# A routed-expert encoder layer: experts add their gated rows into the residual in DRAM, and the last stage only normalises

## What is computed

```python
h = h + parallel_mixer(...)                       # called H2 in the kernel
u = rms_norm(h, norm_ffn_g)                       # called U2
gates = p_grp * (top_p / sum(top_p))              # two experts a token
# tokens sorted by expert, each expert's list padded to blocks of 128 slots
def run_block(args):
    tok, e = args
    xe = x[tok]
    hid = silu(xe @ w_gate[e]) * (xe @ w_up[e])
    return hid @ w_down[e]
y = zeros((T, D)).at[buf_tok].add(yb.reshape(P, D) * buf_gate[:, None])
out = rms_norm(h + y, norm_final_g)
```

## Time and profile before

| | |
|---|---|
| median of 3 runs | 4235.22 us (4228.05 to 4240.24) |
| the profiled execution's own time | 4237.25 us |
| its span, first to last instruction | 4235.1 us |
| attention | from about 540 to 2890 us |
| route | 3291 to 3356 us |
| experts | 3356 to 4060 us |
| combine | 4060.5 to 4235.1 us |
| PE busy in the span | 88% |
| mean granted TensorE clock | 0.935 of full speed |

### The profile page before, as it was taken

One profiled execution on the slowest core, in us unless ns is written; L12 is line 12 of the kernel. 1 busy time (PEld: TensorE's weight loads), 2 busy tenths in 40 slices (PEclk: granted clock), 3 DMA queues, 4 the chain that ended last, 5 costly groups with the idle time before them and its releaser, 6 DMA issues. The chain is left out here.

```text
span 4235.1 us, 60176 instructions
## 1 busy us (share of the span) xinstructions
PE 3738.5 (88%) x16747; PEld 2738.7 (65%) x16748; DVE 2819.2 (67%) x4468; ACT 2366.1 (56%) x4059; POOL 429.1 (10%) x497
## 2 busy tenths in 40 slices
PE   7999856999999999999999999996999499999920
PEld 7989724666666666666666766765777366666610
DVE  5656545888878888777776877743443666666645
ACT  4434303777777777776676766784332155555522
POOL 0000010111111111111011011000000011110123
PEclk9999957999999999999999999998999699999965
DMA  4555574221222211221122022003333277777768
GB/s 161 167 194 194 166 166 160 60 46 26 54 60 60 59 40 28 60 59 42 24 59 60 16 48 60 6 7 141 137 125 113 84 254 249 248 248 248 248 211 295
DMA packets 330198, 495.54 MB, mean 117 GB/s; under 512 B 118791, under 2 KB 261411, under 8 KB 318915
## 3 DMA queue, kind: packets, MB, share of 16 engines
q1 hardware_dynamic: 241798, 359.85, 28.8%
q10 hardware_dynamic: 71888, 73.54, 5.0%
q0 software_dynamic: 16272, 59.25, 4.1%
HBM read 330.84 MB, written 161.78 MB: 116 GB/s over the span
## 5 line engine op out<-in xcount | busy, mean ns | idle before, releaser
L940 ACT ACTIVATE b_p_hi<-b_psS 128x512 fp32r<-128x512 f32 (+1 forms) x1376 | 822.1, 597 | 620.2 <-PE b_psS L1071 579.5
L1071 PE MATMUL b_psS<-b_q,b_k 96*128 96x512 f32 (+3 forms) x3440 | 1053.2, 404 | 53.5 <-ACT b_prob L943 31.6
L988 DVE TENSOR_TENSOR b_p_lo<-b_prob,b_p_hi 128x512 fp32r<-128x512 f32 x1152 | 830.1, 722 | 287.5 <-ACT b_prob L943 248.5
L943 ACT ACTIVATE b_prob<-b_psS 128x512 f32<-128x512 f32 (+1 forms) x1376 | 815.1, 592 | 1.1
L1071 PEld LDWEIGHTS b_psS<-b_q,b_k 96*128 96x128 f32 (+3 forms) x3440 | 629.8, 186 | 285.0 <-ACT b_prob L943 39.2
L996 DVE TENSOR_REDUCE b_mx_s<-b_psM 128x1 f32<-128x512 f32 x1024 | 690.8, 687 | 86.8 <-PE b_psM L1102 66.1
L1102 PE MATMUL b_psM<-b_k,b_q 128*128 128x512 f32 (+1 forms) x1280 | 515.8, 424 | 54.5 <-DMA b_v<-V 39.2
L1094 PE MATMUL b_psO<-b_p_hi,b_v_hi 128*65 128x512 f32 x1280 | 516.9, 404 | 25.8 <-DVE b_p_lo L988 23.9
L1094 PE MATMUL b_psO<-b_p_hi,b_v_lo 128*65 128x512 f32 x1280 | 509.7, 398 | 0.0
L1094 PE MATMUL b_psO<-b_p_lo,b_v_hi 128*65 128x512 f32 x1280 | 509.6, 398 | 0.0
L1102 PEld LDWEIGHTS b_psM<-b_k,b_q 128*128 128x128 f32 (+1 forms) x1280 | 251.8, 197 | 158.2 <-DVE b_mx_s L996 53.1
(11 more groups left out here) (246 smaller groups left out, 5184.9 us busy)
## 6 DMA issues: line engine op xcount, KB each, us to landing
e_w_gu<-w_gate SPq DMA_DIRECT2D x32, 1024.0 KB
e_w_gu<-w_up SPq DMA_DIRECT2D x32, 1024.0 KB
e_w_dn<-w_down SPq DMA_DIRECT2D x32, 1024.0 KB
Y<-e_y ACTq DMA_DIRECT2D x64, 512.0 KB, 5.3
Y<-b_zeros ACTq DMA_DIRECT2D x4, 4096.0 KB, 27.3
a_x_raw<-xallT SPq DMA_DIRECT2D x25, 512.0 KB, 5.0
a_x<-xall SPq DMA_DIRECT2D x25, 512.0 KB, 4.4
c_o<-O SPq DMA_DIRECT2D x24, 512.0 KB, 4.9
```

The lines of the kernel that those rows point to most:

```text
L940: nc.scalar.activation(p_hi[0:kn, (s * NI + j) % NP, :], psS[0:kn, j % 2, :], ACT.Exp)
L943: nc.scalar.activation(prob[0:kn, (s * NI + j) % NP, :], psS[0:kn, j % 2, :], ACT.Exp).then_inc(p_ready, 1)
L988: nc.vector.tensor_tensor(out, prob[0:kn, slot, :], p_hi[0:kn, slot, :].bitcast(F32), ALU.subtract).then_inc(lo_ready, 1)
L1071: m = nc.tensor.matmul(psS[0:kn, j % 2, :], kk[s][0:r, k], qq[s][0:r, q], start=n == 0, stop=n == len(passes) - 1)
```

## The change

`Y` is gone. The residual H2 takes its place as the target: for each block, once its rows are multiplied by their gates, POOL issues an indirect store of 128 rows of 4 KB that adds to the rows of H2 in DRAM. H2 and U2 get 128 rows ahead of the tokens' rows. A slot that only pads a block has token number 0 in `psI` and gets its own row number (0 to 127) instead, so that no row is named twice in one store; its gate is 0. Since a token occurs in two experts' blocks, an add waits until the one before has landed.

- Attention: instead of four stores of 4096 KB there are eight of 128 KB, which clear the new rows of U2 and H2.
- Route: `in_blk` holds two sets of 80 columns, one scaled by the token's number, one by its gate. PE's products have 160 columns, and the result also gives `gates`, per block and row.
- Experts: ACT copies a column of `gates` to `gcur` and scales by it while it takes `psY` out. POOL no longer waits for the landing of its gather, but issues the adds, each four blocks behind the gather ahead of it in its queue. A new count `y_landed` tells ACT that a buffer of `y` is free.
- Combine: SP loads H2 alone, eight tiles deep; ACT and DVE normalise, four results deep.

The core of the diff:

```diff
             for c in range(D // 256):
-                act.dma_start(t["Y"].rearrange("(b p) d -> p b d", p=P)[:, BLOCKS_SURE:, c * 256:c * 256 + 256],
-                              zeros[:, :].unsqueeze(1).broadcast_to([P, BLOCKS - BLOCKS_SURE, 256])).then_inc(y_cleared, 16)
+                for name in ("U2", "H2"):
+                    act.dma_start(t[name][0:P, c * 256:c * 256 + 256], zeros[:, :]).then_inc(cleared_rows, 16)
...
-                        i = nc.tensor.matmul(psI[:, 0:BLOCKS], in_row[:, k, n, :], in_blk[:, k, n, :],
+                        i = nc.tensor.matmul(psI[:, 0:2 * BLOCKS], in_row[:, k, n, :], in_blk[:, k, n, :, :].rearrange("p a b -> p (a b)"),
...
-                    nc.vector.tensor_tensor(in_blk[:, k, part, :], in_blk[:, k, part, :],
-                                            tok[:, part].unsqueeze(2).broadcast_to([P, HN, BLOCKS]),
+                    nc.vector.tensor_tensor(in_blk[:, k, part, 0, :], in_blk[:, k, part, 1, :],
+                                            tok[:, part].unsqueeze(2).broadcast_to([P, HN, BLOCKS]), ALU.mult)
+                    dve.drain()
+                    nc.vector.tensor_tensor(in_blk[:, k, part, 1, :], in_blk[:, k, part, 1, :],
+                                            gate[:, part, 2 + k].unsqueeze(2).broadcast_to([P, HN, BLOCKS]),
                                             ALU.mult).then_inc(places_ready, 1)
...
-            nc.vector.tensor_copy(idx[:, :], psI[:, 0:BLOCKS])
+            nc.vector.tensor_copy(gates[:, :], psI[:, BLOCKS:2 * BLOCKS])
+            nc.vector.tensor_scalar(pad[:, :], psI[:, 0:BLOCKS], 0.0, row_id[:, 0:1], ALU.is_equal, ALU.mult)
+            dve.drain()
+            nc.vector.tensor_tensor(idx[:, :], psI[:, 0:BLOCKS], pad[:, :], ALU.add)
...
-                pool.wait_ge(x_loaded[s], 16 * j + 16)
+            def add(b, s, added):
+                if added is not None:
+                    pool.wait_ge(y_stored[1 - s], added)
+                pool.sem_inc(y_landed, 1)
+                nc.gpsimd.tensor_copy(to[:, s:s + 1], idx[:, bass.ds(b, 1)]).then_inc(to_ready, 1)
+                pool.wait_ge(to_ready, b + 5)
+                pool.sem_inc(pool_carrier, 1)
+                pool.wait_ge(y_ready, b + 5)
+                pool.sem_inc(pool_carrier, 1)
+                pool.indirect_dma_start(t["H2"], bass.IndirectOffsetOnAxis(to[:, s:s + 1], 0), y[:, s, :], None,
+                                        compute_op=ALU.add).then_inc(y_stored[s], 16)
...
+            with pool.Fori(3, BLOCKS // 2) as j:
                 with pool.If(j < pairs + 1):
-                    body(2 * j, j, 0)
+                    gather(2 * j, j, 0)
                 with pool.If(j < pairs):
-                    body(2 * j + 1, j, 1)
+                    add(2 * j - 4, 0, 16 * j - 32)
+                    gather(2 * j + 1, j, 1)
+                    add(2 * j - 3, 1, 16 * j - 16)
...
-                act.wait_ge(y_stored[s], 16 * j + 16)
-                nc.scalar.activation(y[:, s, :], psY[:, :, :].rearrange("p b n -> p (b n)"), ACT.Copy).then_inc(y_ready, 1)
-                act.wait_ge(y_ready, b + 2)
-                act.dma_start(t["Y"][bass.ds(b * P, P), :], y[:, s, :]).then_inc(y_stored[s], 16)
+                act.wait_ge(y_landed, b + 2)
+                nc.scalar.activation(gcur[:, s:s + 1], gates[:, bass.ds(b, 1)], ACT.Copy)
+                act.drain()
+                nc.scalar.activation(y[:, s, :], psY[:, :, :].rearrange("p b n -> p (b n)"), ACT.Copy,
+                                     scale=gcur[:, s:s + 1]).then_inc(y_ready, 1)
...
+            for T in range(N):
+                if T >= HS:
+                    sp.wait_ge(res_ready, T - HS + 1)
+                sp.dma_start(h[:, T % HS, :], t["H2"][bass.ds(T * P + P, P), :]).then_inc(h_loaded[T % HS], 16)
...
+                nc.vector.scalar_tensor_tensor(res[:, T % RS, :], h[:, T % HS, :], rs[:, T:T + 1], g_fin[:, :],
                                                ALU.mult, ALU.mult).then_inc(res_ready, 1)
...
+            def stats(T):
+                act.wait_ge(h_loaded[T % HS], 16 * (T // HS) + 16)
+                nc.scalar.activation(junk[:, :], h[:, T % HS, :], ACT.Square, accum_out=ss[:, T:T + 1])
+                act.drain()
+                nc.scalar.activation(std[:, T:T + 1], ss[:, T:T + 1], ACT.Sqrt, scale=1.0 / D,
+                                     bias=eps[:, 0:1]).then_inc(std_ready, 1)
...
+            for T in range(N):
+                stats(T)
+                if T >= 1:
+                    store(T - 1)
+                act.drain()
```

More of the change, by code:

```diff
@@ L1507, in _, with stage_route @@
             l_turn(N - 1)
-EXPERT_AT, NEW_AT, TARGET_AT, SLOT_AT, PAIRS_AT, STORED_AT = [k * BLOCKS for k in range(5)] + [4 * BLOCKS + 1]
+EXPERT_AT, NEW_AT, TARGET_AT, SLOT_AT, PAIRS_AT, STORED_AT, ADDED_AT = [k * BLOCKS for k in range(5)] + [4 * BLOCKS + 1, 4 * BLOCKS + 2]
 WS = 4
-def stage_route(nc, t, logits, picks, eb, idx):
+def stage_route(nc, t, logits, eb, idx, gates):
     with ExitStack() as ctx:
@@ L1605, in _ @@
             pe.wait_ge(both_ready, 1)
-            pe.wait_ge(loaded, 16 * 5)
+            pe.wait_ge(loaded, 16 * 6)
             for h in range(2):
@@ L1793, in stage_experts @@
         w_dn = sb("w_dn", [P, WS * HC, D])
-        cur = sb("cur", [P, 2], U32)
+        cur, to = sb("cur", [P, 2], U32), sb("to", [P, 2], U32)
+        gcur = sb("gcur", [P, 2])
         x = [sb(f"x{s}", [P, D]) for s in range(2)]
@@ L2063, in stage_combine @@
-        y_loaded = [sem("y_loaded0"), sem("y_loaded1")]
-        h_loaded = [sem("h_loaded0"), sem("h_loaded1")]
-        sum_ready, std_ready, res_ready = sem("sum_ready"), sem("std_ready"), sem("res_ready")
-        res_stored = [sem("res_stored0"), sem("res_stored1")]
-        block = ctx.enter_context(nc.Block())
-        def over_tiles(engine, body):
-            with engine.Fori(0, N // 2 - 1) as j:
-                for s in range(2):
-                    body(2 * j + s, j, s)
-            for s in range(2):
-                body(N - 2 + s, N // 2 - 1, s)
@@ L2078, in is_last @@
-        def is_last(T):
-            return isinstance(T, int) and T == N - 1
+        h = sb("h", [P, HS, D])
+        junk = sb("junk", [P, D])
+        ss, std, rs = sb("ss", [P, N]), sb("std", [P, N]), sb("rs", [P, N])
+        res = sb("res", [P, RS, D])
+        g_loaded, eps_ready = sem("g_loaded"), sem("eps_ready")
+        h_loaded = [sem(f"h_loaded{s}") for s in range(HS)]
+        std_ready, res_ready = sem("std_ready"), sem("res_ready")
+        res_stored = [sem(f"res_stored{s}") for s in range(RS)]
@@ L2146, in _ @@
-            act.wait_ge(eps_ready, 1)
-            stats(0, 0)
-            def body(T, j, s):
-                if not is_last(T):
-                    stats(T + 1, 1 - s)
-                act.wait_ge(res_ready, T + 1)
-                act.dma_start(t["out"][bass.ds(T * P, P), :], res[:, s, :]).then_inc(res_stored[s], 16)
-            over_tiles(act, body)
-            for s in range(2):
-                act.wait_ge(res_stored[s], 16 * (N // 2) + 16)
+                nc.scalar.activation(std[:, T:T + 1], ss[:, T:T + 1], ACT.Sqrt, scale=1.0 / D,
+                                     bias=eps[:, 0:1]).then_inc(std_ready, 1)
@@ L2160, in hymba_trunk, with store @@
+            def store(T):
+                act.wait_ge(res_ready, T + 1)
+                act.dma_start(t["out"][bass.ds(T * P, P), :], res[:, T % RS, :]).then_inc(res_stored[T % RS], 16)
+            act.wait_ge(eps_ready, 1)
+            for T in range(N):
+                stats(T)
+                if T >= 1:
+                    store(T - 1)
+                act.drain()
+            store(N - 1)
+            for s in range(RS):
+                act.wait_ge(res_stored[s], 16 * (N // RS))
 def hymba_trunk(nc, t):
```

126 lines of the change are left out of this document (47 added, 79 removed).

## The result

The changed kernel takes **4131.41 us** (median of 4 runs, 4128.55 to 4133.64) against 4237.73 us for the kernel before beside it (4 runs): ratio 0.9748, 95% interval 0.9721 to 0.9774, faster. Its profiled execution took 4129.44 us, of which the span is 4127.6 us. The table cuts both spans at the same instructions, each worked out from the starts and durations of rows of the timeline.

A forecast was written before the change was run, and what follows sets the result against it. PE was taken to bound experts, ACT's zeroing stores the start of attention, and moving bytes the combine. From 4237.25 us, -28.7 + 6 + 4 + 3.5 - 94.6 = -109.8 gave 4127.4, forecast 4126; range 4100 to 4205.

The forecast's parts named there:

- Attention: Start of attention: eight small zeroing stores free ACT's queue, 32.0 - 3.3 = 28.7 us gained, bounds 27 to 30.
- Route: Route: wider products and a third DVE product cost +6; +6.8 at PE's half clock, +4.3 if DVE is the bound.
- Cost zero: Experts, steady state: an add takes 6.8 us, under the 9.4 at which the adds become slower than PE; no cost.
- the forecast's +4 at this expert: Experts, the one expert with a single block: weights arrive later under the adds' load and PE waits, +4 us.
- The addition's price: Experts: one add takes 5.3 + 1.5 = 6.8 us, a store plus one pass of bytes; upper bound 10.1.
- Tail: End of experts: an unloaded add's 1.5 us more, plus POOL's issue of 0.95 and its waits, +3.5 us.
- Combine: Combine: 25.7 MB at 347 GB/s gives 80 us instead of 174.6, gain 94.6; bounds 71 to 91 us.
- the slow adds: Rival, experts: adds of 10 to 11 us are slower than PE, +40 to +100, so 4165 to 4225; chance 0.22.
- the case that it ends slower: Rival, experts: addition costs DMA time, adds over 11.1 us, 4357 at 13; chance 0.12 including 0.02 within 0.3%.
- the combine at 305 GB/s: Rival, combine: stays at 305 GB/s or ACT and DVE bind, 96 us, so 4142; inside the first case's 0.62.
- the small stores that block: Rival, attention: the large stores' price on ACT was not the cause, small ones block too, 4154; "little for it".
- The mark named for "wrong": Experts: wrong if POOL's waits name the adds and PE shows idle time for `xT_ready` or `y_ready` in every block.

The follow-up runs named there:

- the kernel with both edits: Changed kernel with TensorE's `y_ready` wait ahead of the two others and DVE's register load behind its `e_xT` copy: 4121.45 us, 4112.79 us when run again.
- one edit: Changed kernel with only the `y_ready` wait moved ahead (4124.17 us), or only DVE's register load moved behind its `e_xT` copy (4123.54 us).
- experiment 1: Changed kernel with TensorE's wait for `y_ready` ahead of the waits for `wd_ready` and `hT_ready` instead of behind them: 4124.17 us, ratio 0.9719.
- experiment 10: Changed kernel with only the 80 columns of row numbers multiplied in the route, the gate columns left out and gates set to zero: 4133.74 us (one run).

## Why the prediction came out as it did

*Attention, right.* The stall fell by 28.9 us where 28.7 was forecast, at the place named. The sum takes 3.3 us for the eight small issues, near 0.378 us each. They took 0.39 to 0.47 us each, and ACT's idle time there is 3.08 us. The cause of the rest of the 33.5 us stays open; it is within the 8 us by which this stretch differs between profiles.

*Route, right in size, by the alternative that was put second, and in part by luck.* The forecast took +6 between "+6.8 if PE stays at its half clock" and "+4.3 if it rises". PE rose and DVE is the bound: from the first one-hot group on it is +4.5 (29.63 against 25.17). The other 1.8 lie ahead of the groups, where nothing was forecast. DVE waits 0.95 us longer for its tables, of which there is a sixth now (3.74 us, for `r_row_id`, against 2.79 before), and 1.0 us longer for PE's products `r_psT` (5.47 against 4.46, at a mean granted clock of 0.53 against 0.66); two copies that went give 0.17 back.

*Experts, the step that failed.* The prediction said "Cost zero" for the steady state, and asked only whether the adds' landing keeps under 9.4 us. That question was answered rightly: the landing (median 7.6, forecast 6.8) never stopped PE or ACT. But the prediction went from "the adds are not the bound" to "PE loses nothing", and looked for late data alone. Here PE was 99.14% busy, so whatever lengthens a block by 0.1 us shows. What the runs put in its place, of 22.6 us: 3.3 for the place of the `y_ready` wait alone and 9.7 for DVE's slow register load, 14.0 together, and some 8.6 that remain in the kernel with both edits. Of these, PE's two waits for weights are 4.6 us more than before (12.7 against 8.0; the second of them, at the one-block expert, 5.4 against 1.74). That is the forecast's +4 at this expert. In the changed kernel itself it stayed at 1.8, and it rose as the blocks got quicker: 2.8 and 3.6 with one edit, 4.5 and 5.4 with both. Some 3 us are the 0.05 us a block by which PE's first product of `e_psY` still comes later than before (experiment 1). About 1 us is not placed.

*The addition's price, near.* It was bounded at 4.8 to 10.1 us and taken as a store plus one pass of bytes, 1.5 us. The addition costs 2.3 us of landing and raises the DMA share by 0.12, as much as the whole plain store (0.59 to 0.71 to 0.83). So here an accumulating row occupies the engines for about two plain rows. The Trainium skill (Collectives: The Full Stack, the section on the bandwidth ceiling) puts the reducing collective at half the rate of the copying one, since the add reads two sources. By the shares, the trace agrees with that ratio. The two rivals that rested on a dearer addition did not come about: the median landing of 7.6 us is under the 9.4, though single adds took up to 13.0.

*Tail, right.* +4.3 for +3.5.

*Combine, right mechanism, term mis-sized by 14 us.* "25.7 MB / 347 GB/s" carried over the rate of the kernel before. The rows moved at 413 GB/s with a share of 1.03, above the upper bound of 400 that was named for them. The forecast gave "if these regular rows run faster than gathers" as the condition. That is not shown: with two buffers the same regular rows moved at 279 GB/s with a share of 0.78, that is 358 at a share of 1. Shown is that more transfers in flight raised the rate from 279 to 413 GB/s; the form of the transfers was not tried apart from that.

*The rivals.* The slow adds, the case that it ends slower, the combine at 305 GB/s and the small stores that block are all excluded by the rows above. The mark named for "wrong" was half right: POOL's waits do name the adds (283.0 us), but PE has no idle time for `xT_ready` or because of them. What it had in every block was the pause that `y_ready`'s wait makes by its value, although the count had long been reached.

## What to carry to other kernels

Where an engine is busy 99% of a loop, count what a change does to every wait and register load on its path and on that of the engine just ahead: two delays of 0.05 and 0.15 us a block on average cost 14 us together in 64 blocks, where the forecast had 4 for the whole stage. Put waits that are long satisfied ahead of the one that comes last, and load a register where its engine is idle anyway; both edits together gave 14 us back. Take a transfer's rate from a stretch with as many transfers in flight and of the same form, and expect an accumulating store to cost the DMA engines twice a plain one.

## What was not expected of the hardware

- **Register loads.** DVE's read of one number from SBUF takes 0.31 us, but mostly 0.9 to 1.4 us where it begins beside the start of GpSimd's indirect gather issue while an accumulating store is under way (28 of 28 in the second profile of the changed kernel). Beside the gather's issue with no store under way, none of 31 was slow. With plain stores the two never met, so whether it takes the addition or any store is open.
- **The wait on a count.** Of three waits ahead of one matmul only the second was late. With the third on `b + 4` and not on `b + 1` as the others, and behind them, PE started 0.24 us after the late result; with that wait in front, 0.15; with `b + 1` in all three, 0.10 (the last in the kernel before).
- **The clock.** In the route PE stayed at half clock (0.50, 1.2 GHz) for 21 us of products of 80 columns without a pause, before and in experiment 10. In the changed kernel, with products of 160 columns and no pause from 3305.20 to 3314.46, the granted clock was 0.50 up to 3310 and 0.97 from there to 3315, and behind pauses of 1.15 and 1.68 us it was still 1.00 and 0.96 of 2.4 GHz. So twice the columns cost the route nothing that shows.
- **The rate.** Loads and stores of whole 4 KB rows moved 413 GB/s together with eight tiles deep, and 279 with two, at shares of 1.03 and 0.78; gathers, loads and stores, two deep, had moved 305 at 0.88.
